# Low parts of the weight pieces between two attentions: a GpSimd subtraction becomes a ScalarE negation and an accumulating DMA

## What is computed

```python
def mla_mixer(h, ...):
    proj = h @ w_in
    ...
    o = causal_block_attention(q, k, v, MLA_QK ** -0.5)
    o = o.reshape(B, S, MLA_HEADS * MLA_V) * jax.nn.silu(z)
    return o @ w_out                      # 512x2048 @ 2048x1024

def nsa_mixer(h, ...):
    q, kc, vc, ks, vs, kw, vw, gl, z = jnp.split(h @ w_in, splits, axis=-1)   # 512x1024 @ 1024x4528
    ...
    return o @ w_out

x = x + mla_mixer(rms_norm(x, norm_g[0]), ...)
x = x + nsa_mixer(rms_norm(x, norm_g[1]), ...)
```

## Time and profile before

| | |
|---|---|
| time, median of 3 runs | 947.98 us (947.86 to 949.41) |
| time of the profiled execution | 949.34 us |
| its span, first to last instruction | 947.5 us |
| mean granted TensorE clock | 0.995 of full speed |
| PE, PEld busy | 923.4 us (97%), 828.6 us (87%) |
| DVE, ACT, POOL busy | 555.0 us (59%), 444.9 us (47%), 399.4 us (42%) |
| MLA attention, its last slots | to about 377 us |
| output and input projection between the attentions | about 377 to 700 us |

### The profile page before, as it was taken

How to read it: one execution, slowest core, us unless ns; L and a number is a source line. 1 busy time by engine, 2 the same in 40 slices (tenths; PEclk the granted TensorE clock), 3 DMA queues, 4 the chain that set the end, 5 groups by cost and what they waited for, 6 DMA issues and landing times.

```text
span 947.5 us, 16413 instructions
## 1 busy us (share of the span) xinstructions
PE 923.4 (97%) x5938; PEld 828.6 (87%) x5938; DVE 555.0 (59%) x1669; ACT 444.9 (47%) x1025; POOL 399.4 (42%) x579
## 2 busy tenths in 40 slices
PE   6998998999999999999999999999999999999998
PEld 6998998999999998888888887888888999999986
DVE  5897877977777876211111115666946666666611
ACT  5457656777777776222343233444344333333410
POOL 2000017987787874133373335666813111111121
PEclk9999998999999999999999999999999999999999
DMA  6322231101111012113272212222220100000001
GB/s 203 116 90 89 90 117 49 49 15 46 49 38 48 24 46 80 55 67 109 86 160 87 83 50 90 85 88 80 66 89 2 45 1 1 1 2 1 2 37 52
DMA packets 39259, 58.90 MB, mean 62 GB/s; under 512 B 8694, under 2 KB 22283, under 8 KB 39179
## 3 DMA queue, kind: packets, MB, share of 16 engines
q1 hardware_dynamic: 39136, 57.84, 19.5%
q10 hardware_dynamic: 42, 0.01, 0.0%
HBM read 55.62 MB, written 2.10 MB: 61 GB/s over the span
## 4 chain that ended last, share of the span: by engine, by line
PE 89%; DVE 5%; ACT 4%; issue 1%; DMA 0%; ACTq 0%; POOL 0%; DVEq 0%; POOLq 0%
PE bank L95 18%; PE bank L96 18%; PE bank L97 18%; PE bank L529 7%; PE bank L1103 4%; PE bank L449 2%; PE bank L458 2%; PE bank L450 2%; PE bank L427 2%; PE bank L1092 2%; PE bank L1206 2%; PE bank L1064 1%; PE bank L1065 1%; ACT w_hi L1348 1%; PE bank L1083 1%
## 5 line engine op out<-in xcount | busy, mean ns | idle before, releaser
L1750 POOL TENSOR_TENSOR w_lo<-w_raw,w_hi 128x2048 fp32r<-128x2048 f32 (+1 forms) x26 | 118.2, 4548 | 152.3 <-ACT w_hi L1505 152.2
L95 PE MATMUL bank<-w_hi,h_hi 128*128 128x512 f32 (+3 forms) x480 | 172.8, 360 | 3.2 <-DVE z_sb L1906 2.0
L97 PE MATMUL bank<-w_hi,h_lo 128*128 128x512 f32 (+3 forms) x480 | 168.8, 352 | 0.0
L96 PE MATMUL bank<-w_lo,h_hi 128*128 128x512 f32 (+3 forms) x480 | 168.8, 352 | 0.0
L95 PEld LDWEIGHTS bank<-w_hi,h_hi 128*128 128x128 f32 x480 | 90.2, 188 | 16.4 <-issue 4.7
L97 PEld LDWEIGHTS bank<-w_hi,h_lo 128*128 128x128 f32 x480 | 90.2, 188 | 11.5
L96 PEld LDWEIGHTS bank<-w_lo,h_hi 128*128 128x128 f32 x480 | 90.3, 188 | 10.2
L1505 ACT ACTIVATE w_hi<-w_raw 128x2048 fp32r<-128x2048 f32 (+1 forms) x26 | 49.2, 1890 | 78.4 <-PE bank L97 78.4
L688 POOL TENSOR_TENSOR o_c<-o_c,o_sw 128x256 f32<-128x256 f32 x16 | 11.6, 726 | 167.3 <-DVE o_c L762 167.3
L529 PE MATMUL bank<-kvr,probT 128*128 128x65 f32 x640 | 80.6, 273 | 0.0
L529 PEld LDWEIGHTS bank<-kvr,probT 128*128 128x128 f32 x640 | 78.6, 192 | 1.3
(11 more groups left out here) (305 smaller groups left out, 2381.2 us busy)
## 6 DMA issues: line engine op xcount, KB each, us to landing
w_raw<-in_nsa_w_in SPq DMA_DIRECT2D x10, 1024.0 KB, 5.1
w_raw<-in_mla_w_in SPq DMA_DIRECT2D x8, 1024.0 KB, 5.1
w_raw<-in_mla_w_out SPq DMA_DIRECT2D x8, 1024.0 KB, 5.1
w_raw<-in_nsa_w_in SPq DMA_DIRECT2D x8, 984.0 KB, 4.9
w_raw<-in_mla_w_uq SPq DMA_DIRECT2D x8, 576.0 KB, 4.1
w_raw<-in_mla_w_ukv SPq DMA_DIRECT2D x16, 256.0 KB, 2.7
w_raw<-in_nsa_w_out SPq DMA_DIRECT2D x4, 1024.0 KB, 5.2
w_raw<-in_mla_w_in SPq DMA_DIRECT2D x4, 704.0 KB, 5.8
```

The source lines that it names most:

```text
L95: nc.tensor.matmul(out, a[0], b[0], start=start, stop=False)
L96: nc.tensor.matmul(out, a[0], b[1], start=False, stop=False)
L97: return nc.tensor.matmul(out, a[1], b[0], start=False, stop=stop)
L1750: nc.gpsimd.tensor_tensor(w_lo[g % 2][:, :, 0:width], w_raw[g % 2][:, :, 0:width], w_hi[g % 2][:, :, 0:width].bitcast(F32), ALU.subtract). ...
```

## The change

ScalarE first writes the negated, rounded weight to `w_lo` (counted by the new `m_negated`), then the rounded weight to `w_hi` as before. GpSimd no longer subtracts; it waits for the negation and issues a DMA that reads the piece from DRAM a second time and adds it to `w_lo` in SBUF (`accum_op=ALU.add`), so that `w_lo` becomes the weight less its high part. The semaphore `m_lo` is gone: PE waits for `m_hi` and for the DMA's landing (`m_added`, one for each buffer), and SP loads piece g over `w_raw` as soon as `m_hi` of piece g - 2 is counted.

```diff
+                m_added = [sem(f"m_added{b}") for b in range(2)]
...
+                def mid_rows(g):
+
+                    w, k0, c0, width = mid[g]
+                    return w.rearrange("(k p) c -> p k c", p=P)[:, k0:k0 + KP, c0:c0 + width]
...
                         if g >= 2:
-                            sp.wait_ge(m_lo, g - 1)
-                        sp.dma_start(w_raw[g % 2][:, :, 0:width],
-                                     w.rearrange("(k p) c -> p k c", p=P)[:, k0:k0 + KP, c0:c0 + width]
-                                     ).then_inc(m_landed[g % 2], 16)
+                            sp.wait_ge(m_hi, g - 1)
+                        sp.dma_start(w_raw[g % 2][:, :, 0:width], mid_rows(g)).then_inc(m_landed[g % 2], 16)
...
                     for j, src in enumerate(first_pieces(nsa_w_out[0], 0, CW)):
-                        sp.wait_ge(m_lo, NM - 1 + j)
+                        sp.wait_ge(m_hi, NM - 1 + j)
...
                         for g in range(OUT_J):
-                            pe.wait_ge(m_lo, g + 1)
+                            pe.wait_ge(m_hi, g + 1)
+                            pe.wait_ge(m_added[g % 2], 16 * (g // 2 + 1))
...
                         width = mid[g][3]
+                        nc.scalar.activation(w_lo[g % 2][:, :, 0:width], w_raw[g % 2][:, :, 0:width],
+                                             ACT.Copy, scale=-1.0).then_inc(m_negated, 1)
                         nc.scalar.activation(w_hi[g % 2][:, :, 0:width], w_raw[g % 2][:, :, 0:width],
                                              ACT.Copy).then_inc(m_hi, 1)
...
                     def mid_low(g):
-                        pool.wait_ge(m_hi, g + 1)
-                        width = mid[g][3]
-                        nc.gpsimd.tensor_tensor(w_lo[g % 2][:, :, 0:width], w_raw[g % 2][:, :, 0:width],
-                                                w_hi[g % 2][:, :, 0:width].bitcast(F32), ALU.subtract).then_inc(m_lo, 1)
+                        pool.wait_ge(m_negated, g + 1)
+                        nc.gpsimd.dma_start(w_lo[g % 2][:, :, 0:mid[g][3]], mid_rows(g), accum_op=ALU.add
+                                            ).then_inc(m_added[g % 2], 16)
```

More of the change, by code:

```diff
@@ L318, in trunk @@
                 m_landed = [sem(f"m_landed{b}") for b in range(2)]
-                m_hi, m_lo, m_done, x1_left, n_left = (sem(n) for n in ("m_hi", "m_lo", "m_done", "x1_left", "n_left"))
+                m_hi, m_negated, m_done, x1_left, n_left = (sem(n) for n in ("m_hi", "m_negated", "m_done", "x1_left", "n_left"))
+                m_added = [sem(f"m_added{b}") for b in range(2)]
                 o_turned, o_hi_made, o_lo_made = sem("o_turned"), sem("o_hi_made"), sem("o_lo_made")
@@ L881, in mid_piece @@
                     def mid_piece(g):
-                        w, k0, c0, width = mid[g]
+                        width = mid[g][3]
                         if g == 0:
```

## The result

The change takes 972.93 us (median of 4 runs, 972.21 to 974.08) against 947.92 us for the kernel before on the same chip: the ratio is 1.0263, with a 95% interval of 1.025 to 1.0276. It is slower by 25.0 us, where 32 were forecast. The profiled execution has a span of 972.2 us (before 947.5) and a mean granted TensorE clock of 0.989 (before 0.995).

The account below looks back on a forecast made before the run. PE was taken to bound the 26-piece stage and ScalarE's copies the attention's last slots; 949.3 + 3.7 (negations) + 27 (accumulating DMA) + 1 (piece 9) = 981.0, forecast 980 us as median, range 952 to 1080.

Parts of the forecast that it names:

- The reading of the profile before: PE bounds 377 to 690 us, ScalarE's copies the attention's last slots; subtractions hidden, 4 us and more spare per piece.
- GpSimd's subtractions: Removing GpSimd's 26 subtractions takes away 118 us of work, worth 0, since nobody on the path waited for them.
- The negations in the tail: In the attention's last slots, two more ScalarE instructions on the chain, pieces 0 and 1: 2 x 1.85 = +3.7 us.
- The bound of 3.8: Upper bound in us for the two negations in the attention's last slots; the lower was 0, if the chain had slack.
- The other 24 negations: ScalarE's negations between 390 and 690 us, delaying what is queued behind by 1.9 us; priced at 0 by themselves.
- A: Time from the negation's end to the accumulating DMA's landing; taken as 12 us, costing +27 us over 24 pieces.
- The prediction's own reckoning: Cost of A over 24 uneven steps: 1 us at A = 9, 8 at 10, 17 at 11, 27 at 12.
- The plain load's row: Plain load of the same piece, 5.1 us issue to landing; by it alone A would be 7.7, the sum 952.
- SP's earlier reload: SP's reload waits only for the high copy, starting 4.5 us sooner; worth 0, but runs beside the new DMA.
- Piece 9: Its DMA falls when w1k and w1v fill the DMA engines for 12 us, so A is 13 there: +1 us.
- GpSimd held up by DVE: Rival: DVE holds up GpSimd's descriptor writing in the input projection, up to 5 us more, 985; chance 0.05.
- The signs to look for: Paired ScalarE copies, projection 3 to 4 us later, PE waits of 2 to 5 us, ScalarE +49, GpSimd -118 us.

Follow-up runs that it names:

- the plain copy: The change with GpSimd's DMA copying the piece over w_lo instead of adding (low parts wrong): 953.59 us, ratio 1.0062 to the kernel before.
- pieces 9 and 10 too: The change with GpSimd subtracting pieces 0, 1, 9 and 10, and SP's reload waiting for the complete low part: 953.79 us, ratio 1.0065.
- the later reload: The change with SP reloading w_raw only after the accumulating DMA of piece g - 2 has landed: 963.6 us, ratio 1.0165.

## Why the prediction was right, and where its sizes were off

*The reading of the profile before* held. The tail was bound by ScalarE's copies and the middle by PE, with GpSimd's subtractions hidden and some 4 us of spare time per piece.

*The negations in the tail, forecast +3.7.* Their own part is 3.6 us, in the chain at both places and in the fall of the plain copy's profile from 7.2 to 3.6. The term missed the clock: where it fell behind PE's longer idle time, the same instructions cost 7.2. The bound of 3.8 was wrong for that reason; I had taken PE's work behind the copies as constant. The two runs that isolate the two instructions give 6.3 (alone) and 5.6 us (with the plain copy) in the median.

*The other 24 negations, 0*: measured 0.0008 [-0.0002, 0.0017] of the time by themselves.

*GpSimd's subtractions, 0*: its busy time fell by 85 us and not by 118, since the 26 issues count as busy with 1.3 us each, 34 us. Nobody waited for either.

*A = 12 us, forecast +27*: the mechanism held, with PE waiting at the starts of pieces for a low part that lands too late. Its size was off. A is 10.5 us: 0.3 to the issue, 2.4 fixed, 6.2 for the data (5.2 forecast) and 1.6 from the shared engines (2.6 forecast); the 2.4 are what remains of the 8.6 us beside 6.2. The 1.7 us on top for GpSimd's descriptors and the adding were too much: 1.0 of it went into the data, and the rest wasn't there. The prediction's own reckoning gives 8 us at A = 10 and 17 at 11, so about 12.5 at 10.5. Measured are 19.1 - 5.2 = 13.9 without pieces 9 to 12. The Trainium skill, "Collectives: The Full Stack", section "The bandwidth ceiling: the fold count and why AG ≠ RS ≠ AR", says for the collectives' transfers that the adding kind runs at about half the rate of the copying kind, since the add reads two sources; it doesn't speak of a local one such as this. The trace agrees with the rate, with 200 to 215 GB/s against 405 to 410; the reason no run tests. The plain load's row, by which the sum would have been 952, is what the plain copy showed (953.59) and not the change.

*SP's earlier reload, 0 by itself*: right as the prediction counted it, inside A; held back, it gave 9.3 us in the median.

*Piece 9, forecast +1*: this is the term with the largest error for its size. The slide beside `w1k` and `w1v` is about 5 us, and subtracting only pieces 9 and 10 gave 4.0 back. I had only doubled the data time of one piece. But three pieces' DMAs and their reloads share the engines with the 1,664 KB of `w1k` and `w1v`, from 473 to 511 us, and landings there are 12.6 us in the median, with `w1v` at 15.8 (before 11.4).

*GpSimd held up by DVE*: the Trainium skill, "SBUF — State Buffer", section "Who interferes with whom", would have some DVE copies hold up the writing of descriptors. The issue on GpSimd took 1.28 us in the output projection and 1.33 in the input projection, medians, at most 1.50, so the trace shows no hold of the issue beyond 0.2 us, and the landings in the two stages are alike (10.1 us in the median of both, leaving out pieces 8 to 11). No run was made without DVE's work.

*The signs to look for*: the two copies in a row, the later projection (7 us, though, and not 3 to 4), PE's waits ahead of about every other piece (0.2 to 2.2 us, not 2 to 5), ScalarE's busy time (46 us more, 49 forecast) and the unchanged length behind mark 3 (+0.4 us) all came. So did the rhythm in pairs where PE waits: the two steps from 421.93 to 445.80 us are 23.9, for A + 2.3 + one step = 10.5 + 2.3 + 11.2 = 24.0. The note that the granted clock might fall in the gaps was among the ways to be wrong; it did fall, and it should have been a term of the sum.

Two errors thus stood against each other: 13 us too many for A (27 against 14), and some 8 too few for the clock in the tail and for pieces 9 to 12. The mechanism was right, but that the total came within 7 us of the measured 25.0 is in part luck. Still open is why PE's waits bring a fall of the clock in one execution and not in another, which moves such times by 1 to 3 us.

## What to carry to other kernels

A DMA that adds into SBUF is not a plain load with a flag: here it held the engines for 6.2 us against 2.9, so it has to fit into the spare time per piece together with everything else that moves then, and the first thing to look for is which plain transfer its new waits set free beside it. When work goes onto an engine that the chain passes through, count its length in full, but do not count on getting it back by taking such work away. And where PE had no gaps and now gets them, ask what the granted clock does behind them, and give it a term of its own.

## What the runs showed of the hardware that I had not expected

The granted clock fell behind idle times of a few us. With PE busy 3.47 of 6.00 us from 360 to 366 us, it was 0.89 there and 0.50 from 376 to 380 in one kernel, and 1.00 in both stretches with the same 3.47 us in another; runs of that other kernel differ by 3 us with their mean clock. In the middle a fall came behind single waits of 1.9 us (the change), 2.1 and 2.5 (GpSimd subtracting pieces 0 and 1) and 2.4 (pieces 9 and 10 too), and none behind two of 2.2 in the change and one of 2.8 with the later reload. So PE's idle time stood ahead of every one of these falls, but it didn't always bring one, and what decides between the two stays open.

An accumulating transfer of 1.05 MB used 6.2 us of all 16 engines against 2.9 for a plain load of the same rows, and its issue took GpSimd 1.27 to 1.50 us against 0.74 to 0.99 for the plain copy.
